# The input projections of a gated attention and recurrence block: another order of the tiles, and the keys in one tile of 328 columns

## The chip, the cores and the metric

One core of one Trainium2 chip runs the whole network in one launch. The metric is the device time of one execution in microseconds (us), lower is better. All arithmetic is float32; the large products are split in two parts (below) and multiplied in fp32r.

## What is computed

The reference runs two transformer blocks of one kind (`first_block`) and then one block of another kind (`second_block`), on 256 tokens of width 1024. The change touches the first half of the last block alone:

```
xn = rms_norm(h, g_mix) * (1 + sc1) + sh1
proj = xn @ w_in + b_in                                  # 1024 x 5448
q, k, v, qi, ki, wi, xr, yr, gate_a, gate_b = split(proj)
# widths 512, 128, 128, 512, 64, 8, 1024, 1024, 1024, 1024
attn = dsa_attention(q, k, v, qi, ki, wi, rel_bias)      # indexer scores, top 64 keys, softmax
xr = causal_dwconv(xr)                                   # 4 taps
rnn = rg_lru(xr) * gelu(yr)                              # two gates, then a scan over time
merged = sigmoid(gate_a) * (attn @ w_o_attn) + sigmoid(gate_b) * (rnn @ w_o_rnn)
h = h + ga1 * (merged @ w_out)
```

`dsa_attention` first scores keys with 8 small heads (`qi`, `ki`, `wi`), keeps for each query the n_sel = 64 best keys, and attends with 8 heads and 2 key-value heads to those. `rg_lru` makes two sigmoid gates from 128 x 128 blocks, a decay by exp, and runs `h[t] = a[t] h[t-1] + u[t]` along the tokens.

## The kernel before

**Weights.** Every weight matrix is streamed in parts of up to 128 x 2048 floats: SP loads a part into `raw` (4 buffers), ACT copies it to `hi` in fp32r (line 1199), DVE subtracts to get `lo` (line 1634), 3 buffers of each. PE then makes three matmuls for each 128-row block and token half: hi by high activations, lo by high, hi by low (lines 883 to 885). Both token halves of a tile of up to 512 columns accumulate in two PSUM banks. A split of a later part waits until PE is done with the part that had its buffer. A tile of 512 columns has two parts of 24 matmuls; a part is issued in chunks of 12.

**One written order.** The class `Order` makes one list of steps; each engine's program walks the list in that order and issues its share of each step. So an engine never overtakes: a step that waits holds everything behind it on that engine, while the other engines go on. `IN2` is the list for the last block's input projections: name, first column of `w_in`, width, and three strings with the steps put between the four chunks of the tile (`linear` and `named`). When a tile is done its *evacuation* is a step: `project` on DVE adds the bias row and writes to SBUF (line 1584), into one of two staging buffers (`stage2`, in turn) for what is transposed later; for `yr` ACT and DVE take one half each (lines 1151, 1537).

**The steps between chunks.**
- `qi`, `ki`, `q`, `kv`: PE transposes the staged tile (lines 861 and 863), ACT writes the high part, DVE the low part. Heads have 64 rows and PE needs both operands on the same partitions, so keys are duplicated: DVE copies for `ki` (line 1589) and for `kv` (line 1595) before the transpose.
- `h0` to `h6` (`ihead`): PE makes the scores of two indexer heads (line 898), ACT takes relu, DVE multiplies by `wi` and accumulates (line 1769). `top` adds the causal mask, `top0` to `top7` take eight maxima each and strike them out (lines 1783, 1787). `mask` turns the result into an additive mask, and `attend` has POOL (GpSimd) add it to the relative bias, head by head (line 1856).
- `conv`: PE transposes, ACT makes the first tap, DVE three more (line 1624). `gate` (`rgate`): PE multiplies by the gate blocks (line 1036), ACT takes the sigmoid. `rec`: POOL multiplies (line 1962), ACT makes exp, tanh and squares (lines 1332 to 1339), DVE one product (line 1803). `inc`: ACT square root (line 1343), POOL product (line 1967). `scan`: DVE scans (line 1809), POOL multiplies by the gelu (line 1972). `half`: ACT and DVE split the result (lines 1347, 1814). `bias`: POOL issues two DMAs that fill the relative bias over the buffers that the recurrence has left (line 1980). `gelu`: PE transposes, ACT applies it (line 1313). The second number in a name is the block, the first the half of 512 columns.
- `s0` to `s7` (`att`): step i of the attention pipeline. PE transposes the probabilities of head i-3, makes the scores of heads i and i+1 (i even) and the product with the values of head i-5; ACT the exponential of i-1 (lines 1098, 1099); DVE the reciprocal of i-2 and the biased scores of i-1 (lines 1424, 1465); POOL the normalisation of i-2 (lines 1873, 1874).

## Time and profile before

| | us |
|---|---|
| median of 3 runs | 1084.23 (1083.28 to 1085.28) |
| the profiled execution, its own time | 1086.36 |
| its span, first to last instruction | 1084.3 |
| PE busy, share of the span | 95% |
| input projections of the last block | about 648 to 810 of the span |

Times are of the profiled execution, from the start of its span. PE, DVE, ACT, POOL and SP are the five engines. A row of the timeline is a group of instructions of one line; its time runs from the first start to the last end, and in square brackets stands how long the engine was idle before it and what ended that. Consecutive matmuls overlap, so their distance is read from start to start. The granted clock is the share of TensorE's full clock.

### The profile page before, as it was taken

To read this page: it belongs to the slowest core of one execution; us is meant where nothing else is said; L and a number is where in the kernel's file an instruction comes from. 1 tells how busy PE (TensorE), PEld (TensorE's weight loads), DVE (VectorE), ACT (ScalarE), POOL (GpSimd) and SP (SyncE) were. 2 spreads that over 40 slices of the span, in tenths; PEclk is the share of its full clock that TensorE was granted. 3 is DMA by queue.
4 is the path that set the end of the run, shared out by engine and by line. 5 is a ranking of instruction groups with operands and counts; after the bars stand their busy time and mean duration, and the time that the engine had idled before them with its cause. 6 is when DMAs were issued, how large, how long until landed. Compare 5 with 4: busy or idle time off the path is not lost.

```text
span 1084.3 us, 13459 instructions
## 1 busy us (share of the span) xinstructions
PE 1026.4 (95%) x5180; PEld 850.1 (78%) x5180; DVE 732.6 (68%) x986; ACT 585.8 (54%) x842; POOL 115.6 (11%) x168
## 2 busy tenths in 40 slices
PE   6897999999999989899999999997999999999996
PEld 4675878889888777788888878886877788888885
DVE  5567775566346577578888666769766765777753
ACT  6657554444335567544443354577656456676641
POOL 0112140000000022200000011013630000000001
PEclk9999999999999999999999989999999999999998
DMA  9765479555556432389999796535465535554431
GB/s 348 274 170 73 136 202 303 188 181 174 194 175 197 157 113 76 101 287 352 353 325 320 295 317 215 166 121 165 147 213 206 163 112 184 191 193 156 175 136 39
DMA packets 98190, 213.98 MB, mean 197 GB/s; under 512 B 5440, under 2 KB 12880, under 8 KB 94736
## 3 DMA queue, kind: packets, MB, share of 16 engines
q1 hardware_dynamic: 93424, 196.39, 53.2%
q0 software_dynamic: 4416, 16.51, 6.3%
q8 instruction: 42, 0.69, 0.3%
q10 hardware_dynamic: 288, 0.23, 0.1%
q14 instruction: 20, 0.16, 0.0%
HBM read 208.39 MB, written 6.15 MB: 198 GB/s over the span
## 4 chain that ended last, share of the span: by engine, by line
PE 73%; DVE 11%; ACT 8%; issue 4%; DMA 2%; POOL 1%; SPq 0%; DVEq 0%; ACTq 0%; POOLq 0%
PE bank L883 22%; PE bank L885 22%; PE bank L884 22%; ACT hi L1199 4%; DVE lo L1634 4%; PE bank L861 3%; PE bank L898 1%; PE bank L863 1%; ACT junk L1062 1%; DMA raw<-in_w_in_a 1%; DVE early L1465 1%; DVE xres L1508 1%; DMA raw<-in_w_gate_up 1%; DMA early<-in_memT 1%; PE bank L944 0%
## 5 line engine op out<-in xcount | busy, mean ns | idle before, releaser
L1634 DVE TENSOR_TENSOR lo<-raw,hi 128x2048 fp32r<-128x2048 f32 (+1 forms) x164 | 366.9, 2240 | 215.7 <-ACT hi L1199 215.1
L1199 ACT ACTIVATE hi<-raw 128x2048 fp32r<-128x2048 f32 (+1 forms) x164 | 303.7, 1855 | 184.2 <-PE bank L885 144.0
L883 PE MATMUL bank<-hi,xTh 128*128 128x512 f32 (+2 forms) x896 | 346.8, 387 | 2.6 <-DVE lo L1634 2.2
L885 PE MATMUL bank<-hi,xTl 128*128 128x512 f32 (+2 forms) x896 | 337.7, 377 | 0.0
L884 PE MATMUL bank<-lo,xTh 128*128 128x512 f32 (+2 forms) x896 | 337.7, 377 | 0.0
L883 PEld LDWEIGHTS bank<-hi,xTh 128*128 128x128 f32 x896 | 170.6, 190 | 33.7 <-DVE lo L1634 2.8
L885 PEld LDWEIGHTS bank<-hi,xTl 128*128 128x128 f32 x896 | 170.2, 190 | 31.7
L884 PEld LDWEIGHTS bank<-lo,xTh 128*128 128x128 f32 x896 | 170.5, 190 | 28.5
L883 PE MATMUL bank<-hi,hTh 128*128 128x512 f32 x264 | 103.5, 392 | 0.2 <-DVE lo L1634 0.2
L885 PE MATMUL bank<-hi,hTl 128*128 128x512 f32 x264 | 102.8, 389 | 0.0
L884 PE MATMUL bank<-lo,hTh 128*128 128x512 f32 x264 | 102.8, 389 | 0.0
L883 PEld LDWEIGHTS bank<-hi,hTh 128*128 128x128 f32 x264 | 49.6, 188 | 10.7 <-DVE lo L1634 0.6
L885 PEld LDWEIGHTS bank<-hi,hTl 128*128 128x128 f32 x264 | 49.6, 188 | 10.3
L884 PEld LDWEIGHTS bank<-lo,hTh 128*128 128x128 f32 x264 | 49.6, 188 | 10.1
L1646 DVE SCALAR_TENSOR_TENSOR big<-raw,small,big 128x2048 f32<-128x2048 f32 x24 | 56.3, 2345 | 0.0
L1624 DVE SCALAR_TENSOR_TENSOR big<-bank,cols,big 128x255 f32<-128x255 f32 (+2 forms) x100 | 41.2, 477 | 7.6 <-ACT big L1370 7.6
L1062 ACT ACTIVATE junk<-xres 128x512 bf16<-128x512 f32 x32 | 20.3, 634 | 41.4 <-DVE xres L1567 30.6
L1848 POOL TENSOR_TENSOR rms<-rms,small 128x2 f32<-128x2 f32 x9 | 6.4, 713 | 323.4 <-DVE rms L1399 311.4
L861 PE MATMUL bank<-const,nrm 128*128 128x128 f32 x201 | 35.4, 288 | 3.3 <-DVE nrm L1729 1.3
L861 PEld LDWEIGHTS bank<-const,nrm 128*128 128x128 f32 x201 | 27.2, 149 | 10.5 <-DVE nrm L1729 1.3
L1184 ACT ACTIVATE hTh<-bank 128x512 fp32r<-128x512 f32 x22 | 13.2, 599 | 33.4 <-PE bank L863 33.4
L1370 ACT ACTIVATE big<-bank,cols 128x256 f32<-128x256 f32 x44 | 22.4, 561 | 14.2 <-PE bank L863 14.2
(346 smaller groups left out, 1315.2 us busy)
## 6 DMA issues: line engine op xcount, KB each, us to landing
raw<-in_w_gate_up SPq DMA_DIRECT2D x44, 1024.0 KB, 6.4
raw<-in_w_down SPq DMA_DIRECT2D x30, 1024.0 KB, 5.1
raw<-in_w_ada SPq DMA_DIRECT2D x24, 1024.0 KB, 6.2
raw<-in_w_up SPq DMA_DIRECT2D x22, 1024.0 KB, 5.1
raw<-in_w_in SPq DMA_DIRECT2D x21, 1024.0 KB, 5.0
raw<-in_w_out SPq DMA_DIRECT2D x12, 1024.0 KB, 5.1
raw<-in_w_in_b SPq DMA_DIRECT2D x10, 1024.0 KB, 5.1
raw<-in_w_in_a SPq DMA_DIRECT2D x6, 1024.0 KB, 11.9
```

Source lines behind the costliest of these rows:

```text
L861: e.transpose(bank[:, i * 128:(i + 1) * 128], x, ident)
L863: e.transpose(bank[:, n * 128:(n + 1) * 128], blocks[n], ident).then_inc(x_full, 1)
L883: e.matmul(o, sh, h[:, k, :], start=p.first and k == 0, stop=False)
L884: e.matmul(o, sh, lo[:, k, :], start=False, stop=False)
L885: done = e.matmul(o, sl, h[:, k, :], start=False, stop=p.last and k == p.nk - 1)
L1062: e.activation(junk[:, :], x, ACT.Square, accum_out=rms[i][:, 2 * j + t:2 * j + t + 1]).then_inc(squared, 1)
L1184: e.activation(o, view, ACT.Copy).then_inc(x_high, 1)
L1199: e.activation(hi_s[m % SPLITS][:, 0:n], raw[p.at % RAWS][:, 0:n], ACT.Copy).then_inc(hi_made, 1)
L1370: e.activation(cv[:, j, :], x_bank(task)[:, j * 256:(j + 1) * 256], ACT.Identity, bias=CVB(kt + j), scale=CVW(2, kt + j)).then_inc(conv_be ...
L1624: e.scalar_tensor_tensor(out=o[:, j, n:], in0=bank[:, j * 256:j * 256 + 256 - n], scalar=weights[j][n - 1], in1=o[:, j, n:], op0=ALU.mult, ...
L1634: e.tensor_tensor(lo_s[s][:, 0:n], raw[p.at % RAWS][:, 0:n], hi_s[s][:, 0:n].bitcast(F), ALU.subtract).then_inc(lo_made, 1)
L1646: e.scalar_tensor_tensor(out=piece, in0=raw[i % RAWS][:, :], scalar=small[:, k:k + 1], in1=piece, op0=ALU.mult, op1=ALU.add).then_inc(ada_ ...
```

## The change

It moves the tiles and steps, and replaces the tiles `kw` (72 columns: `ki`, `wi`) and `kv` (256 columns) by one tile `kvw` of 328 columns, for which the columns of `w_in_2` and `b_in_2` are put in the order q, qi, k, v, ki, wi, ... before the launch. The duplication of the keys is now part of the addition of the bias (operands read twice by a broadcast), `ki` has a place of its own (`kiT`, in the buffers of the attention's probabilities), and the low part of v follows in the same evacuation.

```diff
-IN2 = [("qi", 768, 512, ["", "", ""]),
-       ("kw", 1280, 72, ["qi0", "qi2", "x1"]),
-       ("xr", 1352, 512, ["ki", "h0", ""]),
-       ("yr", 2376, 512, ["conv00", "h2 conv02", "h4"]),
-       ("xr", 1864, 512, ["gelu00", "gelu02 h6", "gate000 gate002 top"]),
-       ("yr", 2888, 512, ["gate010 gate012 top0", "conv10 top1", "rec0"]),
-       ("q", 0, 512, ["conv12 top2", "gelu10 inc0 top3", "gelu12 scan0"]),
-       ("kv", 512, 256, ["top4", "half0 bias0 q0 gate100 top5", "q2 gate102 gate110 gate112"]),
-       ("gb", 4424, 512, ["kv top6 top7", "rec1 mask", "attend inc1 s0"]),
-       ("gb", 4936, 512, ["s1 scan1", "s2", "half1 bias1"]),
-       ("ga", 3400, 512, ["", "s3", "s4"]),
-       ("ga", 3912, 512, ["s5", "s6", "s7"])]
+IN2 = [("xr", 1352, 512, ["", "", ""]),
+       ("qi", 512, 512, ["conv00", "", "conv02"]),
+       ("kvw", 1024, 328, ["gate000 gate002 qi0", "qi2", "x1"]),
+       ("xr", 1864, 512, ["ki gate010 gate012", "h0", "kv"]),
+       ("yr", 2376, 512, ["rec0 h2", "conv10", "h4 inc0"]),
+       ("yr", 2888, 512, ["gelu00 h6 conv12", "gelu02 scan0 top", "top0"]),
+       ("q", 0, 512, ["gelu10 top1", "half0 bias0 top2", "gelu12 top3 top4"]),
+       ("gb", 4424, 512, ["gate100 gate102", "q0 gate110 gate112", "rec1 q2 top5"]),
+       ("gb", 4936, 512, ["inc1 top6 top7", "scan1 mask attend", "s0"]),
+       ("ga", 3400, 512, ["s1", "half1 bias1 s2", "s3"]),
+       ("ga", 3912, 512, ["s4", "s5", "s6 s7"])]
...
+        kiT = [x[:, 0, :] for x in p_slots[2][0]]
...
-        staged2 = ["qi", "kw", 1352, 2376, 1864, 2888, "q", "kv"]
+        staged2 = [1352, "qi", "kvw", 1864, 2376, 2888, "q"]
...
                 elif kind == "ki":
-                    e.wait_ge(kw_dup, 2)
-                    turned(claim(step), blocks_of(staged2_slot("kw"), 128, 1))
+                    e.wait_ge(acc_dve, in2_tile[1024].d1)
+                    turned(claim(step), blocks_of(staged2_slot("kvw"), 384, 1))
                 elif kind == "kv":
-                    e.wait_ge(kv_dup, 4)
-                    turned(claim(step), blocks_of(staged2_slot("kv"), 256, 2))
+                    e.wait_ge(acc_dve, in2_tile[1024].d1)
+                    turned(claim(step), blocks_of(staged2_slot("kvw"), 0, 2))
...
-                elif kind == "in2" and l == "kv":
-                    s = staged2_slot("kv")
+                elif kind == "in2" and l == "kvw":
+                    s = staged2_slot("kvw")
                     e.wait_ge(acc_dve, t_.d1)
-                    e.activation(v[2][0][:, :, :], s[:, :, 128:256], ACT.Copy).then_inc(v2_high, 1)
+                    e.activation(v[2][0][:, :, :], s[:, :, 256:384], ACT.Copy).then_inc(v2_high, 1)
...
-                if what == "kw":
-                    e.wait_ge(acc_dve, t_.d1)
-                    e.tensor_scalar(wi[:, :, :], s[:, :, 64:72], 8.0 ** -0.5, None, ALU.mult).then_inc(wi_made, 1)
-                    for u in range(2):
-                        e.tensor_copy(s[:, :, 128 + 64 * u:192 + 64 * u], s[:, :, 0:64]).then_inc(kw_dup, 1)
-                elif what == "kv":
-                    e.wait_ge(v2_high, 1)
-                    e.tensor_tensor(v[2][1][:, :, :], s[:, :, 128:256], v[2][0][:, :, :].bitcast(F), ALU.subtract).then_inc(v2_low, 1)
-                    for t in range(2):
-                        for u in range(2):
-                            e.tensor_copy(s[:, t, 256:512].rearrange("p (h u d) -> p h u d", h=2, u=2)[:, :, u, :],
-                                          s[:, t, 0:128].rearrange("p (h d) -> p h d", h=2)).then_inc(kv_dup, 1)
...
+            def project_keys(t_, pair, full, s, row):
...
+                for t in range(2):
+                    e.wait_ge(*full[t])
+                    e.tensor_tensor(s[:, t, 384:512].rearrange("p (h u d) -> p h u d", h=1, u=2), twice(pair[t][:, 256:320], 1), twice(row[:, 256:320], 1), ALU.add)
+                    e.tensor_tensor(wi[:, t, :], pair[t][:, 320:328], row[:, 320:328], ALU.add).then_inc(wi_sum, 1)
+                    e.tensor_tensor(s[:, t, 0:256].rearrange("p (h u d) -> p h u d", h=2, u=2), twice(pair[t][:, 0:128], 2), twice(row[:, 0:128], 2), ALU.add)
+                    e.tensor_tensor(s[:, t, 256:384], pair[t][:, 128:256], row[:, 128:256], ALU.add).then_inc(acc_dve, 1)
+                e.wait_ge(wi_sum, 2)
+                e.tensor_scalar(wi[:, :, :], wi[:, :, :], 8.0 ** -0.5, None, ALU.mult).then_inc(wi_made, 1)
+                e.wait_ge(v2_high, 1)
+                e.tensor_tensor(v[2][1][:, :, :], s[:, :, 256:384], v[2][0][:, :, :].bitcast(F), ALU.subtract).then_inc(v2_low, 1)
```

Three places of the order, before and now. Lines shift a little: the splits are line 1634 before and 1646 now, the bias additions 1584 and 1592, the scan 1809 and 1820.

**DVE, the keys.** `stage` is a staging buffer, `q2yl` the low part of turned queries, `wi` the head weights, `v2l` the low part of v, `bank` PSUM. Before, at the 72-column tile:

```order
L1634 TENSOR_TENSOR lo<-raw,hi 128x2048
L1406 SCALAR_TENSOR_TENSOR q2yl<-bank,q2yh 128x512 x2
L1584 TENSOR_TENSOR stage<-bank,gbc 128x72 x2
L1587 TENSOR_SCALAR wi<-stage 128x16
L1589 COPY stage<-stage 128x2x64 x2
L1634 TENSOR_TENSOR lo<-raw,hi 128x2048
L1406 SCALAR_TENSOR_TENSOR k2Tl<-bank,k2Th 128x256
```

Now, at the 328-column tile:

```order
L1646 TENSOR_TENSOR lo<-raw,hi 128x2048
L1601 TENSOR_TENSOR stage<-bank,gbc 128x128
L1602 TENSOR_TENSOR wi<-bank,gbc 128x8
L1603 TENSOR_TENSOR stage<-bank,gbc 128x256
L1604 TENSOR_TENSOR stage<-bank,gbc 128x128
L1601 TENSOR_TENSOR stage<-bank,gbc 128x128
L1602 TENSOR_TENSOR wi<-bank,gbc 128x8
L1603 TENSOR_TENSOR stage<-bank,gbc 128x256
L1604 TENSOR_TENSOR stage<-bank,gbc 128x128
L1606 TENSOR_SCALAR wi<-wi 128x16
L1608 TENSOR_TENSOR v2l<-stage,v2h 128x256
L1646 TENSOR_TENSOR lo<-raw,hi 128x2048
```

Eight additions, with a full split ahead of them, stand where two additions, a scaling and two copies stood; the four copies and the v part that stood after the queries are gone from there.

**DVE, from the first scan on.** `big` and `nrm` hold the recurrence, `left` the scores that are struck out, line 1537 (now 1541) is DVE's half of a `yr` evacuation. Before:

```order
L1783 MAX small<-left 128x8 x2
L1787 MATCH_REPLACE left<-small,left 128x128
L1787 MATCH_REPLACE left<-small,left 128x256
L1634 TENSOR_TENSOR lo<-raw,hi 128x2048
L1809 SCALAR_TENSOR_TENSOR big<-big 128x256 x4
L1584 TENSOR_TENSOR stage<-bank,gbc 128x512 x2
L1634 TENSOR_TENSOR lo<-raw,hi 128x2048
```

Now:

```order
L1636 SCALAR_TENSOR_TENSOR nrm<-bank,cols,nrm 128x255 x2
L1636 SCALAR_TENSOR_TENSOR nrm<-bank,cols,nrm 128x254 x2
L1636 SCALAR_TENSOR_TENSOR nrm<-bank,cols,nrm 128x253 x2
L1820 SCALAR_TENSOR_TENSOR big<-big 128x256 x4
L1789 TENSOR_TENSOR left<-acc,const 128x128
L1789 TENSOR_TENSOR left<-acc,const 128x256
L1646 TENSOR_TENSOR lo<-raw,hi 128x2048
L1794 MAX small<-left 128x8 x2
L1798 MATCH_REPLACE left<-small,left 128x128
L1798 MATCH_REPLACE left<-small,left 128x256
L1541 COPY stage<-bank 128x512
L1646 TENSOR_TENSOR lo<-raw,hi 128x2048
```

The scan stood right before the evacuation of the queries; now `top`, a split and `top0` stand between the scan and the evacuation of the second `yr` tile, for which PE waits with `gelu10`.

**POOL, the second half and the attention.** `const`, `acc` and `stage` hold the probabilities of heads 0, 1 and 2; `scratch` is the source of the relative bias. Before:

```order
L1856 TENSOR_TENSOR big<-big,left 128x128
L1856 TENSOR_TENSOR big<-big,left 128x256
L1967 TENSOR_TENSOR big<-big 128x1024
L1864 DMA gbc<-in_b_in 128x512
L1856 TENSOR_TENSOR big<-big,left 128x128
L1856 TENSOR_TENSOR big<-big,left 128x256
L1972 TENSOR_TENSOR nrm<-nrm,big 128x1024
L1873 TENSOR_SCALAR const<-const,stat 128x128
L1874 TENSOR_SCALAR const<-const,stat 128x256
L1856 TENSOR_TENSOR big<-big,left 128x128
L1856 TENSOR_TENSOR big<-big,left 128x256
L1980 DMA big<-scratch 128x4x128
```

Now:

```order
L1978 TENSOR_TENSOR big<-big 128x1024
L1983 TENSOR_TENSOR nrm<-nrm,big 128x1024
L1867 TENSOR_TENSOR big<-big,left 128x128
L1867 TENSOR_TENSOR big<-big,left 128x256
L1867 TENSOR_TENSOR big<-big,left 128x128
L1867 TENSOR_TENSOR big<-big,left 128x256
L1875 DMA gbc<-in_b_in 128x512
L1867 TENSOR_TENSOR big<-big,left 128x128
L1867 TENSOR_TENSOR big<-big,left 128x256
L1991 DMA big<-scratch 128x4x128
L1991 DMA big<-scratch 128x4x256
L1884 TENSOR_SCALAR const<-const,stat 128x128
```

The masks of heads 0 and 1 (the first rows of before are head 1's) stood ahead of the two last products of the recurrence and now stand behind them; the issue of the second bias DMA stood behind the normalisation of head 0 and now stands ahead of it.

## Rows read from the trace of the kernel before

**Rows 1.** Page, busy time of each engine over the whole span.
```profile
PE 1026.4 (95%) x5180; PEld 850.1 (78%) x5180; DVE 732.6 (68%) x986; ACT 585.8 (54%) x842; POOL 115.6 (11%) x168
```

**Rows 2.** Waits of PE from 640 to 885 us: in total, times, longest.
```profile
PE bank L861 <- DVE stage L1584: 4.0, 1, 4.0
PE bank L861 <- POOL acc L1874: 2.7, 1, 2.7
PE bank L861 <- DVE stage L1595: 1.9, 1, 1.9
```

**Rows 3.** Windows: length, busy us of PE, PEld, DVE, ACT, POOL, granted clock, DMA.
```profile
740.00:760.00 20.00, 15.60 (x80) 13.50 (x81) 19.34 (x36) 12.24 (x20) 7.32 (x6) 0.91 0.59 176
```

**Rows 4.** Timeline of PE, the 72-column tile: start us, us, engine, line, operation.
```profile
661.25 0.20 PE L883 MATMUL bank<-hi,xTh 128*128 128x72 f32 x1
...
667.76 0.77 PE L883 MATMUL bank<-hi,xTh 128*128 128x512 f32 x1
...
671.80 0.27 PE L861 MATMUL bank<-const,stage 128*128 128x128 f32 x1
```

**Rows 5.** Timeline of PE, twelve 512-column matmuls between two hand-overs.
```profile
726.23 0.48 PE L883 MATMUL bank<-hi,xTh 128*128 128x512 f32 x1
...
729.07 0.49 PE L861 MATMUL bank<-const,stage 128*128 128x128 f32 x3
```

**Rows 6.** Timeline of PE around its wait for the queries and 256-column tile.
```profile
735.47 0.28 PE L883 MATMUL bank<-hi,xTh 128*128 128x256 f32 x1
...
742.53 0.90 PE L861 MATMUL bank<-const,stage 128*128 128x128 f32 x3 [4.03 <-DVE stage L1584]
...
746.71 0.49 PE L861 MATMUL bank<-const,stage 128*128 128x128 f32 x3
```

**Rows 7.** Timeline of PE around its wait in the attention steps.
```profile
789.08 0.44 PE L861 MATMUL bank<-const,acc 128*128 128x128 f32 x2 [2.65 <-POOL acc L1874]
...
797.57 0.38 PE L861 MATMUL bank<-const,stage 128*128 128x128 f32 x2
```

**Rows 8.** Timeline of DVE, 730 to 757 us.
```profile
733.38 0.62 DVE L1783 MAX8 small<-left 128x8 f32<-128x128 f32 x2
...
734.82 0.62 DVE L1783 MAX8 small<-left 128x8 f32<-128x128 f32 x2
...
738.87 2.42 DVE L1809 TENSOR_TENSOR_SCAN big<-big 128x256 f32<-128x256 f32 x4
...
742.40 3.54 DVE L1634 TENSOR_TENSOR lo<-raw,hi 128x2048 fp32r<-128x2048 f32 x1
...
752.29 3.05 DVE L1592 TENSOR_TENSOR v2l<-stage,v2h 128x256 fp32r<-128x256 f32 x1 [0.48 <-ACT v2h L1155]
...
755.81 2.28 DVE L1634 TENSOR_TENSOR lo<-raw,hi 128x2048 fp32r<-128x2048 f32 x1
```

**Rows 9.** Timeline of DVE, the second half's scan.
```profile
773.79 3.21 DVE L1809 TENSOR_TENSOR_SCAN big<-nrm,big 128x256 f32<-128x256 f32 x4 [1.73 <-POOL big L1967]
```

**Rows 10.** Timeline of POOL (GpSimd), 730 to 792 us.
```profile
741.44 2.35 POOL L1972 TENSOR_TENSOR big<-big 128x1024 f32<-128x1024 f32 x1 [4.64 <-DVE big L1809]
...
752.67 2.39 POOL L1962 TENSOR_TENSOR big<-big,nrm 128x1024 f32<-128x1024 f32 x1
764.95 4.41 POOL L1856 TENSOR_TENSOR big<-big,left 128x128 f32<-128x128 f32 x4 [9.89 <-DVE left L1796]
...
779.89 0.47 POOL L1874 TENSOR_SCALAR const<-const,stat 128x256 f32<-128x256 f32 x1
...
785.20 1.56 POOL L1980 DMA_DIRECT2D big<-scratch  x2 [1.67 <-DVE rTl L1814]
```

**Rows 11.** Timeline of ACT, the first half's recurrence.
```profile
718.78 1.91 ACT L1199 ACTIVATE hi<-raw 128x2048 fp32r<-128x2048 f32 x1
...
722.01 1.72 ACT L1332 ACTIVATE big<-big,small 128x256 f32<-128x256 f32 x4
...
725.38 1.10 ACT L1339 ACTIVATE bank<-big 128x512 f32<-128x512 f32 x2
```

More of the change, by code:

```diff
@@ L431, in named @@
     def named(self, name):
-        for kind in ("conv", "gelu", "qi", "ki", "kv", "top", "half", "bias", "rec", "inc", "scan", "gate", "q", "h", "s"):
-            if name.startswith(kind) and name not in ("kv", "ki", "top"):
+        for kind in ("conv", "gelu", "qi", "top", "half", "bias", "rec", "inc", "scan", "gate", "q", "h", "s"):
+            if name.startswith(kind) and name != "top":
                 numbers = tuple(int(x) for x in name[len(kind):])
@@ L1018, in tensor_program @@
                         e.wait_ge(*emptied(("ki",)))
-                    scores([("ihead", h), ("ihead", h + 1)], [(half_of(qy[2], h_), half_of(kT[2], h_, 0)) for h_ in (h, h + 1)], 128)
+                    scores([("ihead", h), ("ihead", h + 1)], [(half_of(qy[2], h_), [y[64 * (h_ % 2):64 * (h_ % 2) + 64, :] for y in kiT]) for h_ in (h, h + 1)], 128)
                 elif kind == "conv":
@@ L1288, in scalar_program @@
                 elif kind == "ki":
-                    high_of(step, kT[2][0][:, 0:1, :], two(x_bank(step), 1), 1.0)
+                    high_of(step, kiT[0], x_bank(step)[:, 0:256])
                 elif kind == "kv":
@@ L1317, in scalar_program @@
                     e.wait_ge(x_full, filled(step))
+                    e.wait_ge(d_park, 16)
                     if half:
@@ L1533, in evacuate @@
                     e.wait_ge(x_full, filled(end_of[before]))
-                    if before == "kw":
-                        e.wait_ge(wi_made, 1)
+                    if before == "kvw":
+                        e.wait_ge(v2_low, 1)
                     e.wait_ge(*full[1])
@@ L1575, in project @@
                     s = sga[:, :, c - 3400:c - 3400 + w]
+                    e.wait_ge(r_low, 2)
                 else:
@@ L1581, in project @@
                 e.wait_ge(d_brow[n % 2], 16 * (n // 2 + 1))
+                row = gbc[:, n % 2 * 512:n % 2 * 512 + w]
+                if what == "kvw":
+                    return project_keys(t_, pair, full, s, row)
                 for t in range(2):
                     e.wait_ge(*full[t])
[L1584 to L1596 removed]
@@ L1753, in vector_program @@
                 elif kind == "ki":
-                    h, lo = kT[2]
-                    low_of(step, lo[:, 0:1, :], two(x_bank(step), 1), h[:, 0:1, :], 1.0)
+                    low_of(step, kiT[1], x_bank(step)[:, 0:256], kiT[0])
                 elif kind == "kv":
@@ L2105 @@
     given = {n: np.ascontiguousarray(v) for n, v in inputs.items()}
+    for name in ("w_in_2", "b_in_2"):
+        x = given[name]
+        given[name] = np.ascontiguousarray(np.concatenate([x[..., 0:512], x[..., 768:1280], x[..., 512:768], x[..., 1280:]], axis=-1))
     given["constants"] = shape_constants()
```

17 lines of the change are left out of this document (10 added, 7 removed).

## The prediction

> **What bounds the kernel now.** The page comes first: PE is busy 95% of the span [rows 1], so only what PE executes, its clock, and the gaps it is left with can move the end. The waits of PE in the stretch of the input projections come second: three stand out, for the evacuated queries, for the duplicated keys, and for the probabilities of head 1 [rows 2]. Third, the windows: from 740 to 760 us DVE is busy for 19.34 of 20 us while PE has 15.60, and the granted clock is 0.91 [rows 3]. There DVE is the bound. Last, the timelines, which give the prices.
>
> A clock loss stands beside the gaps. Twelve 512-column matmuls and the step to a hand-over take 2.84 us at full clock [rows 5]. After the 72-column tile the same twelve take 4.04 us [rows 4]: part of them ran at 1.2 GHz, the lower of the two levels, though PE never waited. After the waits of 4.03 and 2.65 us [rows 6, 7] matmuls also run slow for a while.
>
> **What the change takes away.**
> - *The two narrow tiles.* The 72-column tile lasts 6.51 us with its two hand-overs of about 0.45 each [rows 4], so 5.6 for its 48 matmuls. 24 matmuls of 256 columns take 3.0 (735.47 to 742.53 less the wait) [rows 6], 0.12 each with the step at the end, so 5.9 for 48. The trace has no 328 columns. The bounds are 0.12 of 256 and 0.237 of 512 columns (2.84 / 12); in proportion it is 0.153, so 7.3 for 48. I take that, since both neighbours lie on one line. Saved: 5.6 + 5.9 - 7.3 = 4.2.
> - *The slow clock behind the 72 columns:* 4.04 - 2.84 = 1.2. A stretch of 256 columns had no such effect before PE waited, so I take 328 as safe.
> - *The wait for the queries:* 4.03, and behind it 4.18 (742.53 to 746.71) [rows 6] for work that I estimate at 2.9 (a hand-over, two gate matmuls, twelve of 256 columns): 5.3. It came from DVE: two rounds of maxima at 1.44 us each (733.38 to 734.82), a split, the scan of 2.42 stood ahead of the evacuation [rows 8]. Now two rounds stand there as well, but the queries are transposed two chunks and four gate matmuls later (`q0` in the `gb` tile), some 7 us that cover the evacuation.
> - *The wait for the duplicated keys:* 1.9 [rows 2]. The low part of v, 256 columns, took 3.05 us there [rows 8], because POOL's product ran from 752.67 to 755.06 [rows 10].
> - *The wait for head 1:* 2.65, and 8.49 (789.08 to 797.57) for work that I put at 6.8 (24 wide matmuls by rows 5 and 1.1 for transposes and scores): 4.3 [rows 5, 7].
>
> Together 4.2 + 1.2 + 5.3 + 1.9 + 4.3 = **16.9 us**.
>
> **What it adds.** I laid the new order of each engine against these durations, from the second tile on.
> - *Keys too early.* The last part of the 328-column tile has only 12 matmuls, 1.85 us. The split ahead of the evacuation on DVE waits for the part before it: ACT's copy 1.91 [rows 11], the subtraction 2.28 [rows 8], then eight additions that I estimate at 1.9: 6.1. PE has 1.85 + 2.84 until it transposes `ki`: a wait of 1.5 with the steps between engines. ACT is held at its copy of v for as long; its next split and the gates' sigmoids come later, which costs PE 0.3 before the first indexer heads. The four removed copies and two additions give DVE about as much as the eight additions take.
> - *The first `gelu00`.* POOL's first product now waits for the bias row behind the `xr` tile, ACT's recurrence of 4.5 us (722.01 to 726.48) [rows 11] then holds the first taps and two splits: DVE reaches the `yr` evacuation 1.2 late.
> - *`gelu10`.* Behind the scan POOL multiplies for 2.35. A split that started in such a product took 3.54 instead of 2.28 and ended 2.2 after it (741.44 + 2.35 = 743.79, and 745.94) [rows 8, 10]: DVE and POOL exclude each other there. So scan end + 2.35 + 2.28 + 1.44 + 0.7 for the copy = 6.8 until PE may transpose. PE waits about 2.6, and by the two like waits loses 1.2 to the clock: 3.8.
> - *Head 0's probabilities.* Before, 15.4 us lay between the first mask on POOL (764.95) and the probabilities of head 0 (780.36) [rows 10]. That chain held two splits, the scan, a product and the exponential; now it holds a product, the masks, two splits, ACT's and DVE's part of `half1` and the issue of the bias, 1.56 [rows 10], ahead of the normalisation: about as long, now counted from the end of the second scan. By the order laid out, PE has some 9 us of work left at that moment (three chunks and the scores of heads 2 and 3): a wait of 6.3, bounds 3 and 11. With 1.7 of slow clock, as behind the wait of 2.65: 8.0. What comes after (head 1 and on) is then ready in time.
>
> Together 1.5 + 0.3 + 1.2 + 3.8 + 8.0 = **14.8 us**. The indexer, POOL's bias rows, SP's loads (same number of parts and bytes; a load has a whole part of slack) and the banks (each new claim finds its bank free) hide behind PE; were the loads late, PE would wait for ACT's copies.
>
> **The sum** is 14.8 - 16.9 = -2.1 us. The profiled execution took 1086.36, 2.1 above the median of 1084.23; I carry the difference to the median: **1082.1 us**. What a measurement of this kernel can tell from no change is about 0.2%, 2.2 us, so the forecast sits on that bound.
>
> **The rivals.**
> - *A, the attention wait is mostly covered (about 1078.8).* If POOL does the masks while DVE evacuates, and the recurrence's second half runs earlier than I laid it, head 0 is ready 3 us after PE comes: 3.3 less. For it: POOL was busy 7.32 of 20 us in the crowded window [rows 3]; there is room. Against it: two splits and POOL's operations exclude each other, and the bias issue is in front.
> - *B, POOL's `inc0` product also stops the indexer (about 1084.5).* The scan took 3.21 beside the masks against 2.42 alone [rows 8, 9], though it is no plain subtraction. It reads two SBUF operands, as the accumulation of `ihead` does. In the new order that product starts just as DVE accumulates heads 4 and 5: up to 2.4 more before `gelu00`. The Trainium skill, page "SBUF — State Buffer", section "Who interferes with whom", says that a DVE instruction with two SBUF inputs contends with GpSimd's reads, and that the one that issues second fully blocks. By that rule, this rival's 2.4 us would be paid in full; the trace agrees with it for the subtraction and has no accumulation beside a product.
> - *C, slower (about 1088.6).* The pipeline of the attention is the bound: its first mask stands behind both recurrence products, and `s0` to `s7` are packed into fewer chunks. The price is 3 us more at head 0 (bound 11), 1.5 of a like wait at `s7`, which now follows `s6` with nothing between, and 2 for the bias DMA if head 4's mask reaches POOL before it lands: 6.5 more. It decides once the probabilities of head 0 come over 9 us after PE. For it: rows 10 and the length of the chain; against it: PE's own waits before shift PE, and not that chain, later.
> - *D, the narrow tile keeps the low clock.* Then 1.2 stays: inside the forecast's range.
>
> **Chances.** Forecast 0.50, half of it below -2.2; A 0.18; B 0.10; C 0.22. Faster by over 0.2%: 0.25 + 0.18 = 0.43; within: 0.25 + 0.10 = 0.35; slower: 0.22. The forecast alone spans 1079.5 to 1084.5, from the bounds 0.12 to 0.237 for a matmul (-1.6 to +4.0, the upper end unlikely) and 3 to 11 for the wait. With most of A and C the range is 1077.5 to 1087.5.
>
> **What would show it.** 48 matmuls of 328 columns in about 7.3 us, full clock behind them; a wait of PE for the keys' additions near 1.5 us; no wait of PE for the evacuated queries; a wait before `gelu10` of 2 to 3 us with a split on DVE stretched by POOL; the longest wait at the first transposes of probabilities, for POOL, 6 us. The forecast is wrong if that last wait is under 3 or over 9 us, if matmuls run at the lower clock behind the 328 columns, or if PE waits in the indexer.

## The result and the profile after

The changed kernel takes **1087.41 us** (median of 13 runs, 1085.67 to 1092.84), the kernel before 1084.23; the ratio is 1.0031, 95% interval 1.0019 to 1.0043. That is 3.4 us slower (2.1 to 4.7), where the forecast said 2.1 faster. Below, "1.0013" means a ratio of this kind to the kernel before, and 0.001 is 1.1 us. The experiments ran in several series, in which the kernel before read 1084.8 to 1086.0, so ratios are compared and not the times beside them; a ratio is not the quotient of the two medians either (e3 has 1.0017 where the medians give 1.0006). One of the twelve executions of e6 took 2055 us and is left out of its ratio. The profiled execution took 1087.64 us, its span is 1085.5 [before: 1084.3].

TensorE's waits in the same stretch, as in [rows 2] (in total, times, longest):
```profile
PE bank L863 <- POOL const L1885: 7.3, 1, 7.3
PE bank L863 <- issue: 3.5, 2, 3.0
PE bank L885 <- DVE lo L1646: 2.4, 2, 1.4
PE bank L863 <- POOL stage L1885: 1.8, 1, 1.8
PE bank L863 <- DVE nrm L1741: 1.5, 1, 1.5
PE bank L863 <- DVE stage L1604: 1.5, 1, 1.5
```
All three waits of [rows 2] are gone. In their place stand head 0's probabilities (POOL const, 7.3), two waits named "issue" (`gelu00` and `gelu10`: the profile names no releaser, but DVE's copy of the staged tile ends 0.1 before each) and the keys' additions (DVE stage L1604, 1.5). Of the splits' 2.4, 1.0 is new, at 779.20. The windows, columns as in [rows 3]:
```profile
720.00:740.00 20.00, 19.47 (x91) 15.97 (x90) 17.95 (x34) 10.81 (x17) 2.63 (x1) 0.89 0.42 123
740.00:760.00 20.00, 20.00 (x96) 16.69 (x96) 13.12 (x24) 13.81 (x21) 4.51 (x4) 1.00 0.59 193
780.00:800.00 20.00, 12.69 (x60) 10.02 (x59) 13.16 (x27) 8.71 (x19) 11.57 (x19) 0.83 0.65 212
```
From 740 to 760, where TensorE had 15.60 us of work in 20 [rows 3], it now has 20.00 at full clock. From 780 to 800 it has 12.69: the longest hole now stands 40 us later.

**A measure for the stretch.** From the first transposes of the normalised input to the first transposes of the merge, TensorE does the same job in every kernel here but e14. Of the length of that stretch I take off TensorE's waits inside it; what is left is its own work, slow clock included. This is one execution each, and executions differ by some 2 us, so it tells where time lies; the ratios tell how much.

| kernel | stretch | waits | rest | ratio of the runs, 95% |
|---|---|---|---|---|
| before | 201.2 | 11.6 | 189.6 | 1 |
| changed | 203.0 | 17.3 | 185.6 | 1.0031 (1.0019 to 1.0043) |
| e1, merged keys, nearly the old order | 204.5 | 18.0 | 186.4 | 1.0031 (1.0016 to 1.0046) |
| e13, new order, narrow tiles | 204.5 | 17.0 | 187.4 | 1.0056 (1.0035 to 1.0077) |
| e18, mask first, s3 late | 200.8 | 13.9 | 186.8 | 0.9998 (0.9985 to 1.0012) |
| e19, e18 with products on DVE | 199.1 | 14.5 | 184.6 | 0.9989 (0.9974 to 1.0003) |

In these two executions the change takes 4.0 us off TensorE's work and adds 5.7 us of waits.

**The three places.** TensorE, the 328-column tile (timeline):
```profile
679.11 0.40 PE L885 MATMUL bank<-hi,xTh 128*128 128x328 f32 x1
...
682.82 0.39 PE L885 MATMUL bank<-hi,xTh 128*128 128x512 f32 x1
```
24 matmuls in 3.71 us, 0.155 each, and the 512 columns behind them step at 0.23: no slow clock. Next, `gelu00` on TensorE, then what DVE and POOL did meanwhile:
```profile
718.60 0.87 PE L863 MATMUL bank<-const,stage 128*128 128x128 f32 x3 [2.99 <-issue]
...
722.54 0.63 PE L886 MATMUL bank<-lo,xTh 128*128 128x512 f32 x1
722.97 0.63 PE L887 MATMUL bank<-hi,xTl 128*128 128x512 f32 x1
```
```profile
714.39 0.74 DVE L1780 SCALAR_TENSOR_TENSOR acc<-const,wi,acc 128x128 f32<-128x128 f32 x2
715.05 2.85 DVE L1780 SCALAR_TENSOR_TENSOR acc<-left,wi,acc 128x128 f32<-128x128 f32 x2
717.83 0.68 DVE L1541 COPY stage<-bank 128x512 f32<-128x512 f32 x1
```
```profile
714.77 2.59 POOL L1978 TENSOR_TENSOR big<-big 128x1024 f32<-128x1024 f32 x1 [11.52 <-ACT big L1347]
```
The accumulation that takes 0.74 a head took 2.85 beside the product, and the copy that `gelu00` needs stood behind it. This is not the same in every execution (see e6). Third, head 0, on DVE and POOL:
```profile
774.12 2.82 DVE L1807 SCALAR_TENSOR_TENSOR left<-acc,const 128x128 f32<-128x128 f32 x2
776.87 2.28 DVE L1646 TENSOR_TENSOR lo<-raw,hi 128x2048 fp32r<-128x2048 f32 x1
779.07 1.27 DVE L1592 TENSOR_TENSOR sgb<-bank,gbc 128x512 f32<-128x512 f32 x2
780.27 2.46 DVE L1646 TENSOR_TENSOR lo<-raw,hi 128x2048 fp32r<-128x2048 f32 x1
782.64 0.28 DVE L1469 CUSTOM_DVE_ANT_0 const<-bank,big 128x128 f32<-128x128 f32 x1
...
785.27 1.23 DVE L1825 TENSOR_TENSOR rTl<-nrm,keep 128x1024 fp32r<-128x1024 f32 x1 [2.00 <-ACT keep L1351]
786.42 0.16 DVE L1428 RECIPROCAL stat<-stat 128x2 f32<-128x2 f32 x1
```
```profile
774.04 2.42 POOL L1983 TENSOR_TENSOR nrm<-nrm,big 128x1024 f32<-128x1024 f32 x1 [3.12 <-DVE big L1820]
...
787.08 1.52 POOL L1991 DMA_DIRECT2D big<-scratch  x2 [2.09 <-DVE rTl L1825]
788.64 0.38 POOL L1884 TENSOR_SCALAR const<-const,stat 128x128 f32<-128x128 f32 x1
```
From the mask (774.12) to the normalising (788.64) head 0 passes six queue places: the mask's last operation, a split, the bias additions of a gate tile, a second split, `half1`, the bias load. (L1469 makes head 0's biased scores; the expectations below call this the softening.) `half1` and the load alone hold it from about 784.3, when ACT's exponential is done, to 788.6. TensorE has less to do meanwhile: `s3`, which needs head 0, stands four chunks behind `s0`, where seven stood between them.

### The profile page after: what moved, and what is told of

The parts are those of the page before. It is cut to its first block, busy times and chain, and to the rows that moved or that the text cites. A ratio compares the mean times of both kernels' runs of the same rounds, so it can differ in the third digit from the quotient of the medians.

```text
span 1085.5 us, 13360 instructions
## 1 busy us (share of the span) xinstructions
PE 1022.5 (94%) x5132; PEld 844.9 (78%) x5132; DVE 733.3 (68%) x984; ACT 582.1 (54%) x840; POOL 115.6 (11%) x167
## 4 chain that ended last, share of the span: by engine, by line
PE 70%; DVE 11%; ACT 9%; issue 5%; DMA 3%; POOL 1%; DVEq 0%; SPq 0%; ACTq 0%; POOLq 0%
PE bank L885 21%; PE bank L887 21%; PE bank L886 21%; ACT hi L1202 4%; DVE lo L1646 4%; PE bank L863 3%; PE bank L900 1%; DMA raw<-in_w_in_a 1%; PE bank L865 1%; ACT junk L1064 1%; DVE early L1469 1%; DMA raw<-in_w_in 1%; DVE xres L1512 1%; DMA raw<-in_w_gate_up 1%; PE bank L1038 1%
## 5 line engine op out<-in xcount | busy, mean ns | idle before, releaser
L1646 DVE TENSOR_TENSOR lo<-raw,hi 128x2048 fp32r<-128x2048 f32 (+2 forms) x164 | 367.4, 2243 | 216.5 <-ACT hi L1202 215.8
L1202 ACT ACTIVATE hi<-raw 128x2048 fp32r<-128x2048 f32 (+2 forms) x164 | 303.4, 1853 | 191.9 <-PE bank L887 145.6
L885 PE MATMUL bank<-hi,xTh 128*128 128x512 f32 (+2 forms) x880 | 342.1, 389 | 5.0 <-DVE lo L1646 3.4
L887 PE MATMUL bank<-hi,xTl 128*128 128x512 f32 (+2 forms) x880 | 333.4, 379 | 0.0
L886 PE MATMUL bank<-lo,xTh 128*128 128x512 f32 (+2 forms) x880 | 333.2, 379 | 0.0
L885 PEld LDWEIGHTS bank<-hi,xTh 128*128 128x128 f32 x880 | 167.1, 190 | 35.9 <-DVE lo L1646 4.2
L887 PEld LDWEIGHTS bank<-hi,xTl 128*128 128x128 f32 x880 | 166.5, 189 | 31.7
L886 PEld LDWEIGHTS bank<-lo,xTh 128*128 128x128 f32 x880 | 167.0, 190 | 28.4
```

The source lines that it names most:

```text
L885: e.matmul(o, sh, h[:, k, :], start=p.first and k == 0, stop=False)
L886: e.matmul(o, sh, lo[:, k, :], start=False, stop=False)
L887: done = e.matmul(o, sl, h[:, k, :], start=False, stop=p.last and k == p.nk - 1)
L1202: e.activation(hi_s[m % SPLITS][:, 0:n], raw[p.at % RAWS][:, 0:n], ACT.Copy).then_inc(hi_made, 1)
L1646: e.tensor_tensor(lo_s[s][:, 0:n], raw[p.at % RAWS][:, 0:n], hi_s[s][:, 0:n].bitcast(F), ALU.subtract).then_inc(lo_made, 1)
```

## The experiments

**Merge and order apart.** e1 has the keys as one tile and, as far as the tiles allow, the old order; with one tile fewer some steps stand elsewhere (`top4` ahead of the queries' evacuation, `s3` five chunks behind `s0` instead of seven). e13 has the new order and the narrow tiles.
```diff
# e1 (order of the kernel before, tile "kvw")
+("kvw", 1024, 328, ["qi0", "qi2", "x1"]),
+("xr", 1352, 512, ["ki", "h0", "kv"]),
...
# e13 (new order, tiles "kw" and "kv")
+("kw", 1280, 72, ["gate000 gate002 qi0", "qi2", "x1"]),
...
+("kv", 512, 256, ["gate100 gate102", "q0", "gate110 gate112"]),
```


> The 328-column tile alone: it takes the place of the 72-column tile, and the other tiles keep the order of before; the steps that lay in the 256-column tile move into the two gb tiles. Theory 1 (the merge is worth the 5.4 us that the prediction gave it, and the order eats it): 48 matmuls of 328 columns in 7.3 to 7.5 us, no matmuls at the lower clock behind them, the wait for the duplicated keys gone, and a time 3 to 8 us below the kernel before (1076 to 1081). Rival (the merge itself costs: keys evacuated too early, the wait for it): within 2 us of the kernel before, with a wait of PE over 1.5 us behind the 328 columns.

Measured: 1088.29, 1.0031. Its waits:
```profile
PE bank L863 <- DVE stage L1592: 5.6, 1, 5.6
PE bank L863 <- POOL acc L1885: 4.0, 1, 4.0
PE bank L863 <- POOL const L1885: 2.3, 1, 2.3
PE bank L863 <- POOL stage L1885: 1.8, 1, 1.8
PE bank L900 <- DVE p2l L1408: 1.8, 1, 1.8
PE bank L863 <- DVE stage L1604: 1.5, 1, 1.5
```
The queries' wait grew from 4.0 to 5.6, head 1's from 2.7 to 4.0, and head 0 waits 2.3 where it waited for nothing. At the keys TensorE waits 1.5 and 1.8, where the wait for the duplicated keys of 1.9 is gone. So TensorE's saving (189.6 to 186.4) came back twice, as 6.4 us of waits. Not all of that is the merge. DVE now makes `top4` between the scan and the queries' evacuation:
```profile
744.81 0.59 DVE L1794 MAX8 small<-left 128x8 f32<-128x128 f32 x2
...
746.21 1.29 DVE L1592 TENSOR_TENSOR stage<-bank,gbc 128x512 f32<-128x512 f32 x2
```
These 1.4 us are about what the queries' wait grew by, and `s3` has two chunks less of cover. No run has the merge with these steps where they were.

> The other half of the change: the new order with the keys still in two narrow tiles (72 columns for the indexer's key and weights, 256 for the keys and values behind the queries), both in the order of columns of the kernel before. With before (1084.2), the merge in the old order (1088.3) and the changed kernel (1087.4) it completes the table of order and merge. TensorE has 4.2 us more matmul time than in the changed kernel. Theory 2 (the chain of DVE, ScalarE and GpSimd from the recurrence and the indexer to head 0 bounds the stretch, TensorE's time in front of it is filled from its waits): the waits (17.3 us in the changed kernel, 11.6 before) fall to 11 to 14 and the time is 1085 to 1088, no more than 1 us over the changed kernel. If TensorE's own time bounded it: 1091 or more.

Measured: 1090.95, 1.0056, with 17.0 us of waits (head 0: 6.8; `gelu00`: 3.0). The expectation of at most 1 us over the changed kernel was too low (2.7 us by the ratios, whose intervals overlap), that of 11 to 14 us of waits too; the time lies by the other branch, in which TensorE's own time bounds (1091). So the order with the narrow tiles costs 6.1 us (3.8 to 8.4), the merge as placed in e1 costs 3.4, and both cost 3.4. They do not add: in the new order the kernel with the merge is 2.7 us ahead of the one without, though the intervals overlap, and in e1 the merge costs 3.4.

**From mask to head 0.** Each edit is of the changed kernel's table:
```diff
# e2
-"scan1 mask attend"
+"mask attend scan1"
# e3
-"half1 bias1 s2"
+"s2 half1 bias1"
# e4: e2 and e3
# e6: e3, and
-"scan1 mask attend", "s0"
+"mask attend s0", "scan1"
# e7
-["s1", "half1 bias1 s2", "s3"] ... ["s4", "s5", "s6 s7"]
+["s1", "s2 half1 bias1", ""] ... ["s3", "s4", "s5 s6 s7"]
```


> The changed kernel with mask and attend ahead of scan1. Theory 1 (the 7.3 us wait for head 0's probabilities comes from the scan, 2.4 us, and from POOL's product that stops the making of the mask, 2.2 us): both leave the chain, the wait falls to 2 to 4 us, and the time falls by 3 to 6 us against the changed kernel. Rival (half1 and the issue of the bias set when head 0 is ready): the recurrence gets later by what the mask gets earlier, the wait stays above 6 us and the time within 1.5 us.

> The changed kernel with s2 ahead of half1 and bias1, so that POOL normalises head 0 before it issues the bias, and ACT and DVE do not split the recurrence first. Theory 1 (chain from the mask): head 0 is 3 to 4.5 us earlier, since 789.5 less 785.3 lay behind the exponential of head 0; the wait falls to 3 to 4 us, the time by 2 to 5 us. Rival (the wait moves on to head 1 or to head 4's mask, for the bias lands later): a new wait of 2 us or more at the next transposes, and a time within 1.5 us of the changed kernel.

> Both moves together. Theory 1: the wait for head 0 is gone or under 1 us, no slow clock behind it, and the time is 6 to 9 us below the changed kernel (1078.5 to 1081.5). Rival (the rest of the attention pipeline, s3 to s7 packed close, is the bound): less than 4 us, with the waits moved to the later heads.

Measured: e2 1087.48 (1.0021), head 0 waits 8.1; e3 1086.55 (1.0017), 4.8; e4 1085.72 (1.0002, 0.9984 to 1.0020), 4.1. The mask alone is made 4 us earlier and wins nothing there: the splits are still ahead of the softening. `half1` and the bias load are the part of the queue that TensorE does feel. In e3 and e4 new waits of 0.7 and 1.6 stand at the probabilities of a later head: the rival's mechanism. e4 is 3.1 us ahead of the changed kernel by the ratios, short of the 6 to 9 expected, and its interval just meets that kernel's.

> The changed kernel with head 0's step right behind the mask (mask attend s0, then the scan), and the second half's correction and bias load behind head 2's step as in e3. Theory 1 (head 0 is late because its softening stands on DVE behind the next tile's split and accumulations, and its normalising behind the bias load on GpSimd: two queue places, about 6 and 2 us): softening of head 0 at about 776 instead of 782.6, head 0's transposes wait under 3 us instead of 7.3, time 1081 to 1084. Theory 2 (the work ahead of the mask is what is late and DVE is full): DVE's split of the next tile moves behind the softening, TensorE waits for that split instead (1.0 us becomes 3 to 5), time 1085 to 1087.

Measured: 1087.44 (1.0010, 0.9992 to 1.0027). The softening started at 781.45, not 776: POOL's scan product and masks stretched a split on DVE to 3.59. Head 0 waits 4.8, TensorE waits for no split there, and neither theory is right as stated. This run shows one thing more. Up to `gelu00` its order is the changed kernel's, and its product starts at the same place, 0.11 into an accumulation, but here POOL was held and DVE was not:
```profile
712.79 0.75 DVE L1780 SCALAR_TENSOR_TENSOR acc<-left,wi,acc 128x128 f32<-128x128 f32 x2
```
```profile
712.50 3.26 POOL L1978 TENSOR_TENSOR big<-big 128x1024 f32<-128x1024 f32 x1 [11.51 <-ACT big L1347]
```
`gelu00` waits 0.94 instead of 2.99, and `gelu10` 3.28 instead of 0.53. In the profiles of e2, e3, e4, e7 and e18, whose order is also the same there, `gelu00` waits 3.0 to 3.1. So the 2.85 is not fixed by the order, and where it stays away (here and in e5) TensorE waits at `gelu10` instead.

> The changed kernel with only TensorE given other work at head 0's place: step s3, which transposes head 0's probabilities, comes two parts of 12 matmuls (5.7 us) later, and the steps behind it closer together. Theory 1 (the wait of 7.3 us is a delay of one chain in a queue that has other work): wait at head 0 about 1.5 us, no slow clock behind it, time down by 5 to 7 us to 1080 to 1082. Theory 2 (DVE, ScalarE and GpSimd bound the stretch from the mask to the merge as a whole: heads 0 to 7 follow each other every 3 to 6 us whatever TensorE does): the wait moves to the heads behind it (heads 2 to 7, or the recurrence's and the merge's splits), their sum stays at 9 to 11 us, time 1086 to 1088.

Measured: 1086.14 (1.0013). Head 0 no longer waits, and head 1 does:
```profile
793.99 0.69 PE L863 MATMUL bank<-const,acc 128*128 128x128 f32 x2 [5.92 <-POOL acc L1885]
```
The edit also contains e3's (`s2` ahead of `half1`), which the expectation leaves out; e3 alone left 4.8 at head 0. The stretch has 14.0 us of waits instead of 17.3 and is as long as before, 203.0, in this execution. Giving TensorE other work in front of head 0 moves most of the wait one head on.

**The indexer and POOL's product.**
```diff
# e5
-"h4 inc0" ... "gelu00 h6 conv12"
+"h4" ... "gelu00 h6 inc0 conv12"
# e8: e5, e7, and "mask attend s0", "scan1" of e6
```


> The changed kernel with one step moved: the input product of the recurrence's first half (inc0) goes from the part before gelu00 to the part behind the last indexer heads. Theory 1 (DVE and GpSimd stop each other: the product of 2.59 us at 714.77 held an indexer accumulation for 2.85 us instead of 0.74, and the copy of the staged tile behind it): the accumulation of head 4 takes 0.7 again, gelu00's wait falls from 2.99 to about 1 us and the slow clock behind it (granted clock 0.89 in 720 to 740) goes; the stage (first transposes of z to the first transposes of the merge, 202.95 us in the changed kernel's profile) is 1 to 3 us shorter only if what TensorE wins there is not waited for again in front of head 0. Theory 2 (the stretch is bound by the chain of DVE, ScalarE and GpSimd up to head 0's probabilities, so time won by TensorE earlier comes back there): gelu00's wait falls all the same, head 0's wait (7.3) grows by as much, the time stays at 1087 +- 1.5.

Measured: 1088.90 (1.0032). DVE at the accumulation of head 4, TensorE at `gelu00` and `gelu10`, DVE's split and POOL's product behind the scan:
```profile
714.52 0.75 DVE L1780 SCALAR_TENSOR_TENSOR acc<-left,wi,acc 128x128 f32<-128x128 f32 x2
...
727.16 4.38 DVE L1646 TENSOR_TENSOR lo<-raw,hi 128x2048 fp32r<-128x2048 f32 x1
```
```profile
715.97 0.52 PE L863 MATMUL bank<-const,stage 128*128 128x128 f32 x3 [0.93 <-issue]
...
733.68 0.58 PE L863 MATMUL bank<-const,stage 128*128 128x128 f32 x3 [4.24 <-issue]
```
```profile
726.75 2.65 POOL L1983 TENSOR_TENSOR big<-big 128x1024 f32<-128x1024 f32 x1 [3.31 <-DVE big L1820]
```
The collision is gone (0.75), `gelu00` waits 0.93, and from its transposes to the next ones (`gelu02`) TensorE takes 4.69 us (715.97 to 720.66) where the changed kernel takes 7.34 (718.60 to 725.94): the slow clock behind the 2.99 us of wait had cost 2.65 more. But `gelu10` now waits 4.24 instead of 0.53. It hangs on scan, split (4.38 beside POOL's product), maxima and copy, one behind the other on DVE. Counted from the start of the stretch they are 1.1 us earlier, and TensorE is there 4.8 earlier. One reason is that ACT's table load and square root (1.28 and 1.06) moved with the step, ahead of the first taps of `conv12`: DVE waits 2.3 us for those. The time stays, as theory 2 says, but the wait came back at `gelu10` and not at head 0, which waits 7.30 as before.

> e5, the steps of e6 and the late s3 of e7 together. If the waits in front of gelu00 and head 0 are separate and neither is bound by a full engine: about 1077 to 1080, faster than both kernels. If each gives its time back further on: 1084 to 1087.

Measured: 1087.31 (1.0028). The waits are 4.2 before `gelu10` and 6.4 before head 1: the time was given back further on.

**The products on DVE.** They take 1.2 us there.
```diff
 # DVE
+elif kind == "inc": ... e.tensor_tensor(ig, ig, rg, ALU.mult).then_inc(inc_made, 1)
 elif kind == "scan": ... done.then_inc(scanned, 1)
+    e.tensor_tensor(gls[half], gls[half], rg, ALU.mult).then_inc(rnn_made, 1)
 # POOL: the same two taken away; e11 moves ig * xcs[half] too
```


> The changed kernel with two of the three products of each half of the recurrence (the input product, 2.4 to 3.5 us on GpSimd, and the product with the gelu after the scan, 2.4) on DVE, right where they are needed. Theory 1 (GpSimd's product and DVE's own SBUF operations stop each other: 2.85 instead of 0.74 at 715.05, 3.8 instead of 2.28 at 729.32, 2.82 instead of 0.62 at 774.12): DVE has 4 x 1.2 = 4.9 us more work but 5 to 6 us less stretching, the chains to gelu00 and head 0 are 1 to 3 us shorter, time 1084 to 1086. Rival (DVE is full at 14.4 of 20 us and every us more on it counts): waits grow by 2 to 5 us, time 1089 to 1092.

> The same move of the two products to DVE in the kernel before, whose waits (4.0 in front of the queries, 2.7 in front of head 1) also stand behind operations that the product stretched (3.54 instead of 2.28, 3.05 instead of 0.7). Theory 1: the queries' wait falls by 1 to 3 us, time 1080 to 1083. Rival: DVE, 19.3 of 20 us busy in 740 to 760, loses 2.4 us there to the added work and the time is 1085 to 1088.

> As e9, with the first product of each half (input gate times convolution, 2.4 us on GpSimd, beside which DVE's split at 701.32 took 4.08 instead of 2.28) on DVE as well. Theory 1: another 1.8 us of stretching goes for 1.2 of work, and GpSimd no longer holds DVE anywhere but in the masks; 1083 to 1086, no slower than e9. Rival: the product now waits in DVE's queue for the gates, and what stands behind it (split, accumulations) waits too: 1 to 3 us slower than e9.

Measured: e9 1087.31 (1.0014, 1.0002 to 1.0025); the same edit of the kernel before, e10, 1087.26 (1.0008, 0.9992 to 1.0025); e11 1092.02 (1.0054, 1.0040 to 1.0068). In e9 the accumulation takes 0.74 and the split behind the scan 2.29 again, so the stretching was POOL's doing; what it gave back about paid for DVE's added work (1.8 us ahead of the changed kernel by the ratios, with intervals that overlap). In e10 the queries' wait grew from 4.0 to 6.1 instead of falling: the rival. The third product costs 4 us. It stands behind a split in DVE's queue and itself waits for nothing; ACT's exponentials write over its input and wait for it:
```profile
703.60 1.71 ACT L1336 ACTIVATE big<-big,small 128x256 f32<-128x256 f32 x4 [2.19 <-DVE big L1811]
```
That is 2.19 us where e9 has 0.71. The rival had the loss, but by another way.

**Which engine has no slack.** e14 repeats the first products of the queries' tile, e15 makes each pair of maxima twice, e16 (changed kernel) and e17 (kernel before) skip the last four rounds of the selection, so they keep 32 keys for each query and not 64.
```diff
# e14
+for _ in range(3 if t_.kind == "in2" and t_.c == 0 and p.first and k == 0 else 0):
+    (the three matmuls of this k, closed)
# e15
+e.max(m8[:, 8 * t:8 * t + 8], seen(left, t))
# e16, e17
+elif kind == "top" and name[0] > 3:
+    pass
```


> The changed kernel with 18 matmuls of 512 columns more for TensorE (4.1 us at 0.228) at the start of the queries' tile, at about 736 to 742; they repeat its first products and change nothing. If DVE's queue up to head 0 bounds the stretch: head 0's wait falls from 7.3 to about 4, and the time grows by under 1.5 us. If TensorE's stream bounds it, by its matmuls or through the gates of the recurrence's second half: the time grows by 3 to 4.5 us and head 0's wait stays.

> The changed kernel with the two MAX8 of each of the 8 top rounds made twice (8 x 0.6 = 4.9 us more for DVE alone, between 731 and 771). If DVE's queue bounds the stretch: head 0's wait grows by 3 to 5 us, or that much appears in front of gelu10 and the splits, and the time grows by 3.5 to 5 us. If it is bound elsewhere, the rounds fall into DVE's idle time (3.0 us before 752.84, 3.1 before 756.61, 2.5 before 761.94): under 1.5 us.

> The changed kernel without the last 4 of the 8 rounds of the indexer's selection on DVE (MAX8 and MATCH_REPLACE, 4 x 1.4 = 5.8 us). If DVE's queue bounds: head 0's wait 7.3 falls to 2 to 4, time down by 3 to 6 us, 1081.5 to 1084.5. If not: the chain to the mask then ends with the recurrence's scan, whose place in DVE's queue is the same, and the time falls by under 1.5 us.

> The kernel before without the same 4 rounds (left out of DVE's 740 to 765). If DVE bounds both, with the merge's matmul time hidden behind it: it gains less than e16 (its waits there are 4.0 and 2.7, its TensorE work 5.3 us more), time 1080.5 to 1083, and e16 is at most 1 us behind it or ahead of it, where the changed kernel is 3.3 us behind the one before. If the order itself costs the 3.3 us: e16 stays 3 us behind e17.

Measured, against the kernel before: e14 1090.33, 1.0046 (1.0025 to 1.0067); e15 1090.32, 1.0041 (1.0021 to 1.0061); e16 1087.70, 1.0009 (0.9987 to 1.0031); e17 1084.97, 0.9998 (0.9979 to 1.0016). From the start of the stretch to head 0's transposes the changed kernel takes 145.4 us, e14 147.4, e15 148.0, e16 143.1. So 4.1 us more for TensorE move head 0 by 2.0, 4.9 more for DVE move it by 2.5, and 5.8 less by 2.3, each in one execution, and executions differ by about that. By the ratios e14 is 1.6 us and e15 1.1 us over the changed kernel, e16 2.4 us under it, with intervals that are wider than that. e14 and e16 lie between the ranges that either reading expected, e15 by its ratio in the one for a bound elsewhere, though its wait at head 0 grew by 2.1 (7.3 to 9.4). In e14 that wait grew too, to 8.3, where one reading had it fall and the other had it stay: what the other engines do for head 0 came later with TensorE's work. So neither engine alone looks like the bound; that about half of a change on either arrives is a reading of single executions and not shown by the ratios. In the kernel before the same 5.8 us less (e17) changed nothing that could be measured, where 1 to 4 us were expected. Of the changed kernel's 3.4 us over the kernel before, 1.2 are left between e16 and e17, whose intervals overlap. A row of DVE in e16 shows why less work there gives only a part:
```profile
768.61 2.44 DVE L1822 TENSOR_TENSOR_SCAN big<-nrm,big 128x256 f32<-128x256 f32 x4 [2.41 <-POOL big L1980]
```
With the rounds gone, DVE waits 2.41 us for the recurrence's product on POOL, which in turn needs ACT's functions and TensorE's gates.

**Together.**
```diff
# e18: e2 and e7
+("gb", 4936, 512, ["inc1 top6 top7", "mask attend scan1", "s0"]),
+("ga", 3400, 512, ["s1", "s2 half1 bias1", ""]),
+("ga", 3912, 512, ["s3", "s4", "s5 s6 s7"])]
# e19: e18 and e9
```


> The changed kernel with the mask ahead of the scan, head 2's step ahead of the second half's correction and bias, and s3 two parts later (e4 and e7 together). If the cost of the new order sits between mask and head 0: waits at head 0 and 1 together under 4 us instead of 7.3, time 1082 to 1084.5, faster than both kernels. If it is spread over the stretch (each wait removed returns at the next handover): 1085 to 1087, like e4 and e7 alone.

> e18 with the recurrence's input product and gelu product on DVE (e9's move), so that no product of 2.4 to 4.4 us on GpSimd stands beside the splits between mask and head 0. If those products are what makes head 0 late (its splits took 2.5 to 3.6 instead of 2.28): 1 to 2 us better than e18. If DVE's queue is what counts: 0 to 2 us worse.

Measured: e18 1085.76 (0.9998), e19 1084.42 (0.9989, 0.9974 to 1.0003), the kernel before beside them 1086.01. In e18 one long wait is left; in e19 it is smaller:
```profile
796.49 0.69 PE L863 MATMUL bank<-const,acc 128*128 128x128 f32 x2 [5.78 <-POOL acc L1885]
```
```profile
794.41 0.44 PE L863 MATMUL bank<-const,acc 128*128 128x128 f32 x2 [3.16 <-POOL acc L1893]
```
By its median e18 lies in the second of the two ranges, but the kernel before read 1.8 us higher in this series than at first; by its ratio it is level with it, and its interval does not meet that of the changed kernel. What the change costs can be had back behind the mask, though not by taking the waits away (5.8 at head 1 where under 4 was expected for both). e19 is better than e18 by 1.0 us by the ratios, as the first reading had it, but their intervals overlap. e19 is 1.2 us ahead of the kernel before, with an interval that reaches to no difference. It is the best version found, not one shown to be faster.

## Why the prediction was wrong

The forecast had 16.9 us going and 14.8 coming. By the two profiles the terms that came are:

| term | forecast | in the changed kernel |
|---|---|---|
| keys too early | 1.5 | 1.45 |
| indexer heads | 0.3 | 0 |
| `gelu00` | 1.2 | 2.99 wait, 2.65 clock |
| `gelu10` | 3.8 | 0.53 |
| head 0 | 8.0 (6.3 and 1.7) | 7.32, 1.02 for the split ahead of it, 1.5 clock |
| transposes of `s7`, behind `p2l` (807.56) | none | 0.77 |
| sum | 14.8 | 18.2 |

The stretch grew by 1.7, so what went was 16.5 (by subtraction), near the 16.9: the narrow tiles (0.155 a matmul against 0.153), the clock behind 72 columns, the waits for queries, duplicated keys and head 1 all went as forecast. Sorted the other way, the forecast has 5.4 off TensorE's own work and 3.3 more waits, the profiles 4.0 and 5.7. Between the runs the difference is 3.4; the 1.7 us between the two are within what single executions differ by, and no row assigns them.

- **The term that was mis-sized most is the added `gelu00`, put at 1.2.** It cost 5.6 in the changed kernel's profile: rival B's mechanism, POOL's product beside the accumulation of a head (0.74 to 2.85), for which I had 2.4 and a chance of 0.10, and a slow clock behind the wait for which I had nothing. That this term alone makes the kernel slower is not shown: in e5 and e6 it is gone (a wait of 0.93 and 0.94, no slow clock), and e5 is no faster. In the same way the product stretched the mask's operation (0.62 to 2.82), which stands in head 0's chain.
- **`gelu10`, put at 3.8, came to 0.53, because it was counted apart from `gelu00`.** Both hang on one sequence of DVE work. Without the collision (e5, e6) `gelu10` waits 4.24 and 3.28; together they were forecast at 5.0 and cost 6.2. `gelu10` cost only 0.53 because TensorE had already waited at `gelu00`.
- **Head 0** was the longest wait, for POOL, 7.3 of a forecast 6.3 and within its bounds. With the split and the clock it cost 9.8 against 8.0. Rival C came nearest in time (1088.6), but hardly by its mechanism: it wanted over 9 us there, its wait at `s7` came with 0.77 of 1.5, and the bias DMA did not delay head 4. The wait of 2 to 3 us before `gelu10` did not come, yet none of the conditions at the end of the prediction, by which it would be wrong, watched `gelu00`'s wait for its copy.
- **Behind these stands the step that failed: the sum.** I took 4.2 us of matmuls and 9 us of waits as gains in full and set single new waits against them, each as if the others stood still. e1, with TensorE's saving and nearly the old order, shows that none of it arrives there; e5 and e8 show a removed wait coming back at the next hand-over; e14 has 4.1 us more, and head 0 moves by half of that in its execution. How much of the 3.4 us belongs to each place stays open; e18 shows that the order from the mask to the merge can give back all of it within the measured interval. A busy share of 95% [rows 1] is an average; in this stretch TensorE's work, DVE's queue and the recurrence share the path.

## What to carry to other kernels

When several engines hand work round a short stage, cost a saving by what its next waiting point gains: lay the arrival of each engine at each handover, before and after, instead of adding removed waits to removed work. In an in-order queue, look what stands between a chain's operations (here a split, a correction and a DMA issue in front of head 0's normalising): moving the last two behind the head's normalising gave 1.5 us (e3, with intervals that overlap), and with the mask ahead of the scan as well the kernel is level with the one before (e4; e18, which has `s3` later too). Where POOL and DVE both read SBUF, place POOL's long products beside DVE work that reads PSUM (the copy took 0.69 beside the product in e6), or check whether DVE does them in half the time (1.2 against 2.4 here), and what then waits for DVE's queue.

## What the hardware showed that was not expected

- A scalar_tensor_tensor on DVE with two SBUF operands is held by POOL's tensor_tensor as a plain subtraction is: 0.74 to 2.85 us beside a product of 2.59. POOL is held too: in e18 the scan product took 4.45 beside two splits, against 2.42 in the changed kernel. The Trainium skill, page "SBUF — State Buffer", section "Who interferes with whom", says that the instruction that issues second is blocked; the rows of the changed kernel and of e18 agree with it.
- Which side is held is not told by the start times of the rows. In the changed kernel and in e6 the product starts 0.11 us after the same accumulation has begun. In the one the next accumulation, 0.28 later, took 2.45 us for its first part; in the other it took 0.35, and the product 3.26 instead of 2.59.
- The price of the granted clock behind a wait differs from place to place: 2.65 us behind a wait of 2.99, about 1.5 behind one of 7.32, and none behind 0.53.
- The same wait does not always bring the slow clock. A wait of 1.8 us for POOL stands between 813 and 821 us in every kernel. From its end to the first transposes of the merge TensorE takes 30.2 to 30.3 us, but 31.8 to 31.9 in e5 (granted clock 0.93 from 820 to 840) and in four other executions: a slow clock that cost 1.6 us. The changed kernel's execution does not have it. Single profiles are no finer than that.
